# Blocks of 64 rows for the expert slots, half-size row moves, and another order of the expert tasks in a fused two-block model on one core

## The chip, the cores and the metric

The kernel runs on one core of a Trainium2 chip. The metric is the device time of one execution in microseconds (us). TensorE is PE in the profile (PEld: its weight loads), VectorE is DVE, ScalarE is ACT, GpSimd is POOL, and SyncE is SP, which here issues the weight loads.

## The reference

256 tokens of 1024 numbers pass through a first block (a mixer of sliding-window attention and gated linear attention, then a gated feed-forward part with a short convolution), and through a second block (a pooling mixer, a dense SwiGLU part, a state-space mixer, and a mixture of experts), all in float32. The change touches the last part only:

```python
t = h.reshape(b * l, d)                              # 256 tokens x 1024
logits = jnp.matmul(t, w_router).astype(jnp.float32) # 8 experts
top_val, top_idx = lax.top_k(logits, TOP_K)          # two experts for each token
gates = jax.nn.softmax(top_val, axis=-1)
...
for e in range(N_EXPERTS):                           # w_gate, w_up: 1024 x 3584; w_down: 3584 x 1024
    y_e = swiglu(t, w_gate[e], w_up[e], w_down[e]).astype(jnp.float32)
    out = out + combine[:, e:e + 1] * y_e            # combine: the gate of a token for e, or 0
```

The result is added to the residual, and a last norm follows.

## The kernel before

**Weights.** All weights come as units of 1 MB (128 partitions x 2048 numbers). SP loads a unit into one of six buffers `raw`; ACT rounds it to `w_hi`, DVE makes the rest `w_lo` = raw - w_hi, and PE multiplies with both parts. A buffer of `raw` comes free when DVE has made `w_lo` (the semaphore `lo_done`); there are three pairs of `w_hi` and `w_lo` (a fourth in small tasks), which come free when PE has used them (`unit_used`). Each engine has its own list of instructions, written out by hand, and semaphores order them between engines.

**Tasks.** Only the chosen experts of a token are computed. The kernel sorts tokens by expert into tasks of at most 128 or at most 64 rows, on the chip, since the counts depend on the data. Experts are split so that three of them have a large task (128 rows): expert 0 and the two others with most tokens. What they have over 128 rows, and the other experts, go into small tasks of 64 rows. A task loads the whole weights of its expert: 42 units. In a large task PE makes three products for each piece of weights (`mm3`); in a small one the high and the low half of 64 tokens lie side by side as 128 rows, and PE makes two (`mm2`). With the data of the runs there are eight tasks, three large and five small. Task 0 is expert 0's large one, and starts before the router's table is known. The small tasks follow, and the two other large ones come last (`n_next`, `n_last`). The engines read the number of tasks from `tasks` into registers, and run the small ones in a loop.

**Slots.** `slot_rows` in HBM has 128 rows for each of up to 16 tasks, with the token's number and its gate in each; a small task uses 64 of its 128. It is first filled with the number of an empty token. DVE works out the row of each token in `slots` (between the splits of task 0), the position list in `positions` and the list of tasks in `task_table`; POOL scatters token numbers and gates to `slot_rows` and reads the table back as `slot_tab`.

**Row moves, all issued by POOL.** `next_rows` gathers the 128 tokens of the next task from `token_rows` while the present task runs; PE transposes them near its end (`turn_rows`). When a task's result is complete, its 128 rows are stored to `result_rows`. During the last task, both results of each token are gathered from `result_rows` by position. Long before, at about 274 us, while the first feed-forward part runs, POOL fills all of `result_rows` (2048 rows) from 128 empty rows of `token_rows`, in one copy from HBM to HBM (L746).

The lines of the rows: L907 are SP's loads, L253 and L262 the splits in halves (large tasks and all earlier parts), L1462 and L2368 whole splits (small tasks), L269 to L271 `mm3`, L275 and L276 `mm2`, L2826 and L2829 the products of the feed-forward part, L1174 ACT's copies out of it, L3079 `turn_rows`, L2303 the low half of a product, L787 the reading of the slot table, L798 `next_rows`' gather.

## Time and profile before

| | us |
|---|---|
| median of 3 runs (lowest, highest) | 1787.6 (1787.14, 1790.38) |
| the profiled execution | 1786.82 |
| its span | 1785.1 |

The span is from the first to the last instruction; the time of the profiled execution is 1.7 us more. Mean granted TensorE clock: 0.989 of full speed. The first block takes up to about 400 us, the second block's parts before the experts up to about 870, the eight tasks the rest.

A row of a timeline gives start, length, engine, line, operation, what it writes and reads, how many instructions are merged in it, and in brackets how long the engine was idle before it and what ended that. A row of waits gives who waited for whom, with the total, the number of times and the longest.

### The profile page before, as it was taken

Reading aid. Unit: us, or ns where it says so; the run is one execution under the profiler, and the core shown is the slowest. Engines: PE = TensorE matmul, PEld = TensorE weight load, DVE = VectorE, ACT = ScalarE, POOL = GpSimd, SP = SyncE. Lnnn points to the kernel's source line nnn. Section 1 sums busy time; section 2 is a strip of 40 time slices with the busy share of each in tenths; the row PEclk is TensorE's granted clock in tenths of the full one; section 3 lists DMA queues with packets and bytes.
Section 4 is the critical chain, followed back from the end, with each engine's and each line's share of the span. In section 5 each row is a group of like instructions: output and inputs, shape, how many; then the busy total and the mean of one; then the engine's idle time right before and its main releaser. Section 6 shows DMA issues by size and latency. Waiting matters only on the chain.

```text
span 1785.1 us, 25176 instructions
## 1 busy us (share of the span) xinstructions
PE 1709.8 (96%) x8774; PEld 1432.4 (80%) x8774; DVE 1465.9 (82%) x1653; ACT 1254.0 (70%) x1490; POOL 188.0 (11%) x230
## 2 busy tenths in 40 slices
PE   9999998999999999999999998998999989999998
PEld 7888887888888899988877776776777777788886
DVE  6686775778766688857799899999999999999997
ACT  6655664556644576666677888888888888877776
POOL 2040050000000000132034100202012020000100
PEclk9999999999999999999999999999999999999999
DMA  9433459754555545433599999999999999999994
GB/s 337 149 111 135 159 199 281 269 197 151 184 193 188 167 165 190 157 127 107 205 349 383 382 421 406 424 422 420 424 420 423 421 420 425 404 396 365 410 383 182
DMA packets 176181, 515.45 MB, mean 289 GB/s; under 512 B 10964, under 2 KB 58450, under 8 KB 161634
## 3 DMA queue, kind: packets, MB, share of 16 engines
q1 hardware_dynamic: 172146, 493.08, 73.2%
q0 software_dynamic: 3808, 21.01, 3.2%
q8 instruction: 51, 0.84, 0.2%
q14 instruction: 32, 0.26, 0.0%
q10 hardware_dynamic: 144, 0.26, 0.0%
HBM read 508.01 MB, written 14.70 MB: 293 GB/s over the span
## 4 chain that ended last, share of the span: by engine, by line
PE 64%; DVE 14%; DMA 10%; issue 7%; ACT 5%; POOL 0%; DVEq 0%; ACTq 0%; SPq 0%; POOLq 0%
PE ps L269 14%; PE ps L271 14%; PE ps L270 14%; PE ps L2826 8%; DVE w_lo L2368 6%; DMA raw<-in_moe_w_gate_dram 5%; PE ps L2829 4%; DMA raw<-in_moe_w_up_dram 3%; DVE w_lo L262 3%; DMA raw<-in_w_ffn_in_dram 2%; DVE w_lo_more L2368 2%; ACT w_hi L1462 2%; PE ps L275 2%; PE ps L276 2%; PE ps L3226 1%
## 5 line engine op out<-in xcount | busy, mean ns | idle before, releaser
L262 DVE TENSOR_TENSOR w_lo<-raw,w_hi 128x1024 fp32r<-128x1024 f32 x517 | 612.0, 1233 | 87.3 <-ACT w_hi L253 85.3
L253 ACT ACTIVATE w_hi<-raw 128x1024 fp32r<-128x1024 f32 x518 | 518.9, 1057 | 169.2 <-PE ps L271 150.8
L2368 DVE TENSOR_TENSOR w_lo<-raw,w_hi 128x2048 fp32r<-128x2048 f32 x165 | 372.3, 2286 | 32.8 <-ACT w_hi L1462 31.6
L1462 ACT ACTIVATE w_hi<-raw 128x2048 fp32r<-128x2048 f32 x165 | 313.7, 1915 | 52.4 <-PE ps L276 23.5
L269 PE MATMUL ps<-w_hi,a 128*128 128x512 f32 (+1 forms) x656 | 259.6, 396 | 3.4 <-DVE w_lo L262 2.3
L271 PE MATMUL ps<-w_hi,a 128*128 128x512 f32 (+1 forms) x656 | 254.3, 388 | 0.0
L270 PE MATMUL ps<-w_lo,a 128*128 128x512 f32 (+1 forms) x656 | 253.8, 387 | 0.0
L2826 PE MATMUL ps<-a,w_hi 128*128 128x512 f32 x704 | 223.1, 398 | 6.9 <-DVE w_lo L262 6.9
L275 PE MATMUL ps<-w_hi,a 128*128 128x512 f32 x420 | 177.3, 422 | 14.6 <-DVE w_lo L2368 12.9
L269 PE MATMUL ps<-w_hi,a_hi 128*128 128x512 f32 (+1 forms) x440 | 170.8, 388 | 2.4 <-DVE w_lo L262 2.1
L276 PE MATMUL ps<-w_lo,a 128*128 128x512 f32 x420 | 170.6, 406 | 0.0
L271 PE MATMUL ps<-w_hi,a_lo 128*128 128x512 f32 (+1 forms) x440 | 169.6, 386 | 0.0
L270 PE MATMUL ps<-w_lo,a_hi 128*128 128x512 f32 (+1 forms) x440 | 169.6, 385 | 0.0
L2829 PEld LDWEIGHTS ps<-a,w_lo 128*128 128x128 f32 x704 | 133.3, 189 | 31.5
L269 PEld LDWEIGHTS ps<-w_hi,a 128*128 128x128 f32 x656 | 123.3, 188 | 31.6 <-issue 4.3
L271 PEld LDWEIGHTS ps<-w_hi,a 128*128 128x128 f32 x656 | 123.1, 188 | 25.7
L270 PEld LDWEIGHTS ps<-w_lo,a 128*128 128x128 f32 x656 | 123.3, 188 | 23.4
L2829 PE MATMUL ps<-a,w_lo 128*128 128x256 f32 x704 | 139.1, 279 | 0.0
L275 PEld LDWEIGHTS ps<-w_hi,a 128*128 128x128 f32 x420 | 83.1, 198 | 45.8 <-DVE w_lo L2368 28.9
L2826 PEld LDWEIGHTS ps<-a,w_hi 128*128 128x128 f32 x704 | 109.5, 190 | 8.6 <-DVE w_lo L262 7.1
L1174 ACT ACTIVATE arena<-ps 128x256 f32<-128x256 f32 x88 | 28.9, 381 | 109.5 <-PE ps L2829 109.5
L275 PE MATMUL ps<-w_hi,a_hi 128*128 128x512 f32 x240 | 96.2, 401 | 8.3 <-DVE w_lo L2368 7.5
(450 smaller groups left out, 2700.6 us busy)
## 6 DMA issues: line engine op xcount, KB each, us to landing
raw<-in_moe_w_gate_dram SPq DMA_DIRECT2D x112, 1024.0 KB, 9.1
raw<-in_moe_w_up_dram SPq DMA_DIRECT2D x112, 1024.0 KB, 9.0
raw<-in_moe_w_down_dram SPq DMA_DIRECT2D x112, 1024.0 KB, 9.8
raw<-in_ssd_w_in_dram SPq DMA_DIRECT2D x24, 1024.0 KB, 5.1
raw<-in_w_ffn_in_dram SPq DMA_DIRECT2D x22, 1024.0 KB, 5.1
raw<-in_w_in_dram SPq DMA_DIRECT2D x21, 1024.0 KB, 6.7
raw<-in_w_ffn_out_dram SPq DMA_DIRECT2D x11, 1024.0 KB, 5.0
raw<-in_dense_w_gate_dram SPq DMA_DIRECT2D x11, 1024.0 KB, 5.2
```

The costliest lines, as they stand in the source:

```text
L253: nc.scalar.activation(w_hi[:, u % SPL, part], raw[:, u % RAW, part], ACT.Copy).then_inc(hi_done, 1)
L262: last = nc.vector.tensor_tensor(w_lo[:, u % SPL, part], raw[:, u % RAW, part], w_hi[:, u % SPL, part].bitcast(F32), ALU.subtract)
L269: nc.tensor.matmul(o, lh, rh, start=start, stop=False, skip_group_check=True)
L270: nc.tensor.matmul(o, lh, rl, start=False, stop=False, skip_group_check=True)
L271: return nc.tensor.matmul(o, ll, rh, start=False, stop=stop, skip_group_check=True)
L275: nc.tensor.matmul(o, l, rh, start=start, stop=False, skip_group_check=True)
L276: return nc.tensor.matmul(o, l, rl, start=False, stop=stop, skip_group_check=True)
L1174: last = nc.scalar.activation(dst[:, fc, :], ps[bank + fc][:, S:2 * S], ACT.Copy)
L1462: nc.scalar.activation(small_part(u, True), raw[:, (M0 + u) % RAW, :], ACT.Copy).then_inc(hi_done, 2)
L2368: nc.vector.tensor_tensor(small_part(u, False), raw[:, (M0 + u) % RAW, :], small_part(u, True).bitcast(F32), ALU.subtract).then_inc(lo_don ...
L2826: nc.tensor.matmul(ps[bank + fc][:, :], w_hi[:, slot, cols], a0_hl[:, kc].rearrange("p a s -> p (a s)"), start=(kc == 0), stop=False, skip ...
L2829: last = nc.tensor.matmul(ps[bank + fc][:, 0:S], w_lo[:, slot, cols], a0_hi[:, kc, :], start=False, stop=(kc == DC - 1), skip_group_check= ...
```

## The change

1. **Packing.** `slot_rows` and `result_rows` have 19 blocks of 64 rows instead of 16 of 128: a small task takes one block, a large one two. `slot_tab` has two numbers for each of 19 windows of 128 rows that begin 64 rows apart; it is read by two copies, the second shifted by a block into the upper 64 partitions. The fill of `result_rows` copies 19 times 64 rows.
2. **Row moves.** A small task's rows are gathered as 64, and its result is stored as 64. Before each gather stands an addition of one column on POOL, and one more before the last gathers.
3. **Order of tasks.** Large, small, large, the other small ones, large: tasks 0, 2 and the last are large. Task 1 and 2 are written out; the loop has one round less.
4. **Table work.** `slots` and `task_table` become pieces (`slots_small`, `slots_large`, `slots`, `task_large`, `task_small`, `task_match`, `task_table`), most of them called behind single splits (`behind`). The formulas differ, since rows are packed otherwise and the order of tasks is another.

Its core (the same renamings for ACT, and the new table formulas beside the first, are left out):

```diff
+WINDOWS = MAX_TASKS + 3
...
-        slot_rows = nc.dram_tensor("slot_rows", (MAX_TASKS * P, 2), F32).ap()
-        result_rows = nc.dram_tensor("result_rows", (MAX_TASKS * P, D), F32).ap()
+        slot_rows = nc.dram_tensor("slot_rows", (WINDOWS * HALF, 2), F32).ap()
+        result_rows = nc.dram_tensor("result_rows", (WINDOWS * HALF, D), F32).ap()
...
-                pool.dma_start(result_rows.rearrange("(i p) d -> i p d", p=P),
-                               bcast(token_rows[S:S + P, :], 0, MAX_TASKS)).then_inc(y_out, 16)
+                pool.dma_start(result_rows.rearrange("(i p) d -> i p d", p=HALF),
+                               bcast(token_rows[S:S + HALF, :], 0, WINDOWS)).then_inc(y_out, 16)
...
-                pool.dma_start(slot_tab.rearrange("p (i c) -> p i c", c=2),
-                               slot_rows.rearrange("(i p) c -> p i c", p=P)).then_inc(tab_out, 16)
+                for n in range(2):
+                    windows = slot_tab[n * HALF:(n + 1) * HALF].rearrange("p (i c) -> p i c", c=2)
+                    pool.dma_start(windows[:, 0:WINDOWS - n], slot_rows[n * HALF:WINDOWS * HALF, :].rearrange(
+                        "(i p) c -> p i c", p=HALF)).then_inc(tab_out, 16)
...
+                def next_rows(i, window, n):
+
+                    pool.wait_ge(tab_out, 48 + 32 * T)
+                    nc.gpsimd.tensor_copy(next_idx, slot_tab[:, window]).then_inc(rows_idx, 2)
                     pool.wait_ge(rows_out, 32)
+                    pool.wait_ge(rows_idx, 2 * i)
+                    nc.gpsimd.tensor_tensor(pad[:, 64:65], pad[:, 65:66], pad[:, 66:67], ALU.add)
+                    nc.gpsimd.indirect_dma_start(m_row[0:n], None, token_rows,
+                                                 bass.IndirectOffsetOnAxis(ap=next_idx[0:n], axis=0)).then_inc(rows_in, 16)
+
+                def store_rows(i, rows, n):
+
                     pool.wait_ge(m_yhi, 2 * i + 2)
-                    pool.dma_start(result_rows[bass.ds(i * P, P), :], y_row).then_inc(y_out, 16)
+                    pool.dma_start(result_rows[rows, :], y_row[0:n]).then_inc(y_out, 16)
                     pool.wait_ge(y_out, i * 16 + 32)
+
+                next_rows(1, slice(4, 5), HALF)
+                store_rows(0, slice(0, P), P)
+                next_rows(2, slice(6, 7), P)
+                store_rows(1, slice(2 * HALF, 3 * HALF), HALF)
+                next_rows(3, slice(10, 11), HALF)
+                store_rows(2, slice(3 * HALF, 5 * HALF), P)
+                with pool.Fori(0, n_loop) as r:
+                    next_rows(r + 4, bass.ds(r * 2 + 12, 1), HALF)
+                    store_rows(r + 3, bass.ds(r * HALF + 5 * HALF, HALF), HALF)
+                next_rows(n_last, bass.ds(n_last * 2 + 4, 1), P)
+                store_rows(n_final, bass.ds(n_final * HALF + 2 * HALF, HALF), HALF)
+                nc.gpsimd.tensor_tensor(pad[:, 67:68], pad[:, 65:66], pad[:, 66:67], ALU.add)
...
+                def slots_small():
+
+                    C.link(nc.vector.tensor_tensor(base, end, parts, ALU.subtract))
+                    C.link(nc.vector.tensor_scalar(base, base, float(HALF), HALF - 1.0, ALU.mult, ALU.add))
+                    C.link(nc.vector.tensor_tensor(by_expert(row), by_expert(rho), bcast(base, 1, T), ALU.add))
+                    C.link(nc.vector.tensor_scalar(shift, row, 2.0 * HALF - 0.5, 2.0 * HALF, ALU.is_gt, ALU.mult))
+                    C.link(nc.vector.scalar_tensor_tensor(row, row, float(HALF), shift, ALU.add, ALU.add))
...
-                def wide_step_lo(i, j, added=None):
+                def wide_step_lo(i, j, added=None, behind={}):
...
                     for u in range(gate_u + 2, up_u + 2):
                         split_lo(dve, M0 + u, 7 * i)
+                        behind.get(u, lambda: None)()
...
-                wide_step_lo(0, 0, slots)
+                wide_step_lo(0, 0, None, {7: slots_small, 9: slots_large, 11: slots})
                 positions()
-                wide_step_lo(0, 1, task_table)
+                wide_step_lo(0, 1, None, {17: task_large, 19: task_small, 21: task_match})
+                task_table()
                 wide_step_lo(0, 2)
...
                 task(0, True)
                 small_head(1)
                 pe.wait_ge(r_tab, 1)
...
-                with pe.Fori(1, n_small) as i:
+                small_task(1)
+                project(0, ps[2], 7 * 2, 2)
+                project(2, ps[6], 7 * 2)
+                pe.wait_ge(m_yhi, 2 * 2)
+                task(2, True)
+                small_head(3)
+                with pe.Fori(3, n_final) as i:
                     small_task(i)
                     small_head(i + 1)
-                small_task(n_small)
-                project(0, ps[2], 7 * n_next, n_next)
-                project(2, ps[6], 7 * n_next)
-                pe.wait_ge(m_yhi, 2 * n_next)
-                task(n_next, True)
+                small_task(n_final)
                 project(0, ps[2], 7 * n_last, n_last)
```

How the instructions stand, at three places. First POOL, at about 262 to 274 us, before:

```order
L732 DMA arena<-in_pool_scale_dram 128x1024
L735 DMA token_rows<-pad 2048x1x64
L737 MEMSET slot_io 128x32
L738 IOTA slot_io 128x16
L740 IOTA slot_io 128x4
L743 DMA slot_rows<-slot_io 128x16x2
L746 DMA result_rows<-token_rows 16x8x16384
```

and after the change:

```order
L733 DMA arena<-in_pool_scale_dram 128x1024
L736 DMA token_rows<-pad 2048x1x64
L738 MEMSET slot_io 128x38
L739 IOTA slot_io 128x19
L741 IOTA slot_io 128x4
L744 DMA slot_rows<-slot_io 64x19x2
L747 DMA result_rows<-token_rows 19x4x16384
```

The last row is the fill: 16 times 8 pieces of 16384 numbers before, 19 times 4 after.

Then VectorE in the first wide step of task 0 (L262, after the change L263, are splits; two rows make a unit), before:

```order
L262 TENSOR_TENSOR w_lo<-raw,w_hi 128x1024 x8
L2303 TENSOR_TENSOR a_lo<-ps,a_hi 128x4x128
L262 TENSOR_TENSOR w_lo<-raw,w_hi 128x1024 x8
L2313 TENSOR_TENSOR arena<-arena,ps 128x512 x2
L2254 TENSOR_TENSOR arena<-arena 128x8
L2255 TENSOR_SCALAR arena<-arena 128x8
L2256 TENSOR_SCALAR arena<-arena 128x8
L2257 SCALAR_TENSOR_TENSOR arena<-arena 128x8
L2258 SCALAR_TENSOR_TENSOR arena<-arena 128x8
L2259 TENSOR_TENSOR arena<-arena 128x48
L2260 TENSOR_REDUCE arena<-arena 128x16
L2261 TENSOR_SCALAR arena<-arena 128x16
```

and after:

```order
L263 TENSOR_TENSOR w_lo<-raw,w_hi 128x1024 x4
L2284 TENSOR_TENSOR arena<-arena 128x8
L2285 TENSOR_SCALAR arena<-arena 128x8
L2286 TENSOR_TENSOR arena<-arena 128x16
L2287 TENSOR_SCALAR arena<-arena 128x16
L2288 SCALAR_TENSOR_TENSOR arena<-arena 128x16
L263 TENSOR_TENSOR w_lo<-raw,w_hi 128x1024 x4
L2292 TENSOR_SCALAR arena<-arena 128x1
L2293 TENSOR_SCALAR arena<-arena 128x8
L2294 TENSOR_SCALAR arena<-arena 128x8
L2295 SCALAR_TENSOR_TENSOR arena<-arena 128x8
L2354 TENSOR_TENSOR a_lo<-ps,a_hi 128x4x128
```

The operations on 128x8 and 128x16 are table work. Before, all twelve stand behind the two products (128x512 x2) and ahead of the next unit; after, five stand behind the first two units of the step, four behind the next two, four further on.

Last POOL in task 0, from the scatters to the gather for the second task, before:

```order
L784 DMA slot_rows<-slot_io,slot_idx 2048x2 x4
L787 DMA slot_io<-slot_rows 128x16x2
L790 TENSOR_LOAD tasks
L790 ISA x2
L801 UNCONDITIONAL_BRANCH
L795 ISA
L795 COPY slot_idx<-slot_io 128x1
L798 DMA arena<-token_rows,slot_idx 128x1024
```

and after:

```order
L785 DMA slot_rows<-slot_io,slot_idx 1216x2 x4
L790 DMA slot_io<-slot_rows 64x19x2
L790 DMA slot_io<-slot_rows 64x18x2
L793 TENSOR_LOAD tasks
L793 ISA x2
L794 TENSOR_LOAD tasks
L794 ISA x2
L795 TENSOR_LOAD tasks
L795 ISA x2
L800 CAST slot_idx<-slot_io 128x1
L803 TENSOR_TENSOR pad<-pad 128x1
L804 DMA arena<-token_rows,slot_idx 64x1024
```

The table is read by two copies, three values are loaded instead of one, and an addition stands between the copy of the indices and the gather, which is of 64 rows.

## Rows read from the trace of the kernel before

**Rows 1.** the page, part 1: busy us, share, instructions.

```profile
PE 1709.8 (96%) x8774; PEld 1432.4 (80%) x8774; DVE 1465.9 (82%) x1653; ACT 1254.0 (70%) x1490; POOL 188.0 (11%) x230
```

**Rows 2.** stretches of the experts: us, busy by engine, PEclk, DMA share, GB/s.

```profile
872.00:1000.00 128.00, 123.83 (x568) 102.04 (x567) 118.95 (x153) 98.76 (x114) 33.47 (x25) 1.00 0.92 346
1000.00:1110.00 110.00, 100.21 (x464) 79.14 (x462) 100.83 (x57) 93.97 (x70) 4.55 (x3) 0.97 1.01 405
...
1217.00:1324.00 107.00, 97.88 (x455) 77.87 (x455) 99.60 (x57) 90.72 (x69) 12.47 (x3) 0.97 1.02 422
...
1538.00:1657.00 119.00, 118.96 (x541) 98.71 (x540) 108.84 (x104) 93.14 (x103) 4.25 (x4) 1.00 0.99 386
```

**Rows 3.** waits of PE, 255 to 345: us in total, times, longest.

```profile
PE ps L2826 <- DVE w_lo L262: 6.9, 1, 6.9
```

**Rows 4.** timeline of ACT: start us, us, what, count, idle before.

```profile
274.50 0.66 ACT L1174 ACTIVATE arena<-ps 128x256 f32<-128x256 f32 x2 [3.55 <-PE ps L2829]
...
291.09 0.66 ACT L1174 ACTIVATE arena<-ps 128x256 f32<-128x256 f32 x2 [3.55 <-PE ps L2829]
...
308.91 2.00 ACT L253 ACTIVATE w_hi<-raw 128x1024 fp32r<-128x1024 f32 x2 [11.59 <-DMA raw<-in_w_ffn_in_dram]
...
333.70 0.66 ACT L1174 ACTIVATE arena<-ps 128x256 f32<-128x256 f32 x2 [3.55 <-PE ps L2829]
```

**Rows 5.** DMA issues, 270 to 275: count, KB each, us from issue to landing.

```profile
raw<-in_w_ffn_in_dram SPq DMA_DIRECT2D x1, 1024.0 KB, 38.1
...
result_rows<-token_rows POOLq DMA_DIRECT2D x1, 35.1
```

**Rows 6.** DMA queues, 280 to 305 (q0: POOL's): packets, MB, share.

```profile
q0 software_dynamic: 124, 8.13, 97.0%
q1 hardware_dynamic: 311, 0.49, 8.2%
```

**Rows 7.** stretches of the first feed-forward part, columns as in rows 2.

```profile
305.00:320.00 15.00, 8.09 (x34) 6.76 (x33) 8.43 (x14) 8.32 (x12) 0.00 (x0) 0.77 0.92 328
```

**Rows 8.** waits of PE, 862 to 1006.

```profile
PE ps L269 <- DVE w_lo L262: 3.9, 2, 1.9
```

**Rows 9.** timeline of PE: turning rows, then tasks' first matmuls.

```profile
980.75 1.03 PE L3079 MATMUL ps<-cst,arena 128*128 128x128 f32 x8
...
997.96 0.39 PE L275 MATMUL ps<-w_hi,a 128*128 128x512 f32 x1
...
1106.08 0.50 PE L275 MATMUL ps<-w_hi,a 128*128 128x512 f32 x1
...
1427.29 0.50 PE L275 MATMUL ps<-w_hi,a 128*128 128x512 f32 x1
...
1535.85 0.50 PE L269 MATMUL ps<-w_hi,a 128*128 128x512 f32 x1
...
1654.98 0.39 PE L269 MATMUL ps<-w_hi,a 128*128 128x512 f32 x1
```

**Rows 10.** timeline of DVE in task 0: the first of each lump.

```profile
910.08 0.15 DVE L2254 TENSOR_TENSOR arena<-arena 128x8 f32<-128x8 f32 x1
...
941.56 0.27 DVE L2271 TENSOR_TENSOR arena<-arena,cst 1x128 f32<-1x128 f32 x1
```

**Rows 11.** waits of DVE, 882 to 950.

```profile
DVE a_lo L2303 <- ACT a_hi L1385: 1.0, 2, 0.6
DVE w_lo L262 <- ACT w_hi L253: 0.2, 1, 0.2
```

**Rows 12.** timeline of POOL in task 0.

```profile
962.01 1.21 POOL L787 DMA_DIRECT2D slot_io<-slot_rows  x1 [5.79 <-DMA slot_rows<-slot_io,slot_idx]
...
971.18 1.16 POOL L798 DMA_INDIRECT arena<-token_rows,slot_idx  x1 [0.81 <-POOL slot_idx L795]
```

**Rows 13.** DMA issues, 970 to 973: count, us to landing.

```profile
arena<-token_rows,slot_idx POOLq DMA_INDIRECT x1, 8.6
```

More of the change, by code:

```diff
@@ L45 @@
 MAX_TASKS = 16
-N_BEFORE, N_LAST, N_TASKS = 16, 19, 20
+WINDOWS = MAX_TASKS + 3
+N_LOOP, N_PAST, N_FINAL, N_LAST, N_TASKS = 16, 17, 19, 20, 21
 UC = 2048
@@ L2151, in _ @@
                 first_e = R[18][:, NE:2 * NE]
-                order, large, rest, parts, end, place, base, swap = (m_tab[:, NE * k:NE * (k + 1)] for k in range(8))
+                order, large, rest, parts, end, place, base, second = (m_tab[:, NE * k:NE * (k + 1)] for k in range(8))
                 over, key = m_tab[:, 64:128].rearrange("p (e f) -> p e f", e=NE), m_tab[:, 128:136]
                 step, over4 = m_tab[:, 136:140], m_tab[:, 160:192].rearrange("p (e k) -> p e k", k=4)
-                rho, whole, left, back = (m_tab[:, 192 + 16 * k:208 + 16 * k] for k in range(4))
-                over3 = m_tab[:, 256:304].rearrange("p (n k) -> p n k", k=3)
+                rho, row, wide_row, shift = (m_tab[:, 192 + 16 * k:208 + 16 * k] for k in range(4))
+                last_row = m_tab[:, 256:257]
+                ordinal, not_two = m_tab[0:1, 272:288], m_tab[0:1, 288:304]
+                later = m_tab[0:1, 304:305]
                 below, same = (m_tab[0:1, 320 + 128 * k:448 + 128 * k].rearrange("p (i e) -> p i e", e=NE) for k in range(2))
@@ new lines, in slots_large @@
+                def slots_large():
+                    C.link(nc.vector.tensor_scalar(last_row, end[:, NE - 1:NE], float(HALF), 4.0 * HALF, ALU.mult, ALU.add))
+                    C.link(nc.vector.tensor_scalar(second, order, 1.0, last_row, ALU.is_equal, ALU.mult))
+                    C.link(nc.vector.tensor_scalar(place, order, 0.5, 3.0 * HALF, ALU.is_lt, ALU.mult))
+                    C.link(nc.vector.scalar_tensor_tensor(place, place, P - 1.0, second, ALU.add, ALU.add))
+                def slots():
+                    C.link(nc.vector.tensor_tensor(by_expert(wide_row), by_expert(rho), bcast(place, 1, T), ALU.add))
+                    C.link(nc.vector.scalar_tensor_tensor(row, rho, 0.5, row, ALU.is_gt, ALU.mult))
+                    C.link(nc.vector.scalar_tensor_tensor(wide_row, rho, 0.5, wide_row, ALU.is_lt, ALU.mult))
+                    C.link(nc.vector.tensor_tensor(R[5], row, wide_row, ALU.add))
@@ new lines, in task_large, with task_small @@
+                def task_large():
+                    C.link(nc.vector.tensor_scalar(later, end[0:1, NE - 1:NE], 2.0, None, ALU.add))
+                    C.link(nc.vector.tensor_scalar(second[0:1], order[0:1], 1.0, later, ALU.is_equal, ALU.mult))
+                    C.link(nc.vector.tensor_scalar(place[0:1], order[0:1], 0.5, 2.0, ALU.is_lt, ALU.mult))
+                    C.link(nc.vector.tensor_tensor(place[0:1], place[0:1], second[0:1], ALU.add))
+                def task_small():
+                    C.link(nc.vector.tensor_tensor(ordinal, iota_row[0:1, 0:MAX_TASKS], ordinal, ALU.subtract))
+                    C.link(nc.vector.tensor_tensor(below, bcast(end[0:1, :], 1, MAX_TASKS), bcast(ordinal, 2, NE), ALU.is_lt))
+                    C.link(nc.vector.tensor_reduce(small_e, below, AX.X, ALU.add))
@@ L2270, in task_table, with task_match @@
+                def task_match():
                     row = iota_row[0:1, 0:MAX_TASKS]
[L2271 to L2272 removed]
                     C.link(nc.vector.tensor_tensor(same, bcast(place[0:1, :], 1, MAX_TASKS), bcast(row, 2, NE), ALU.is_equal))
@@ L2337, in wide_step_lo @@
                         split_lo(dve, M0 + u, 7 * i)
+                        behind.get(u, lambda: None)()
                     product(i, 2 * j + 1)
@@ L2343, in wide_step_lo, with task_end_lo @@
                         split_lo(dve, M0 + u, 7 * i)
-                def task_end_lo(i, more, first=False, n=P):
+                def task_end_lo(i, more, gate_at, n=P):
                     split_lo(dve, M0 + 36, 7 * i)
@@ L2352, in task_end_lo @@
                         tokens_lo(i + 1, n)
-                    dve.wait_ge(tab_out, 32 + 32 * T)
-                    nc.vector.tensor_copy(m_gate, slot_tab[:, 1:2] if first else slot_tab[:, bass.ds(i * 2 + 1, 1)]).then_inc(m_gates, 1)
+                    dve.wait_ge(tab_out, 48 + 32 * T)
+                    nc.vector.tensor_copy(m_gate, slot_tab[:, gate_at]).then_inc(m_gates, 1)
                     for u in range(38, 44 if more else 42):
                         split_lo(dve, M0 + u, 7 * i)
-                def task_lo(i, more):
-                    for j in range(3):
-                        wide_step_lo(i, j)
-                    task_end_lo(i, more)
                 def whole_lo(i, *units):
```

114 lines of the change are left out of this document (53 added, 61 removed).

## The prediction

> **What bounds the kernel now.** First the page: TensorE is busy for 1709.8 of 1785.1 us, the others clearly less [rows 1]. So an edit pays where TensorE waits, or where it runs no faster than its data come. The table of stretches gives the second kind. In the five small tasks TensorE is busy for 98 to 100 us of 107 to 110, while the DMA share is 1.01 to 1.02 at 405 to 422 GB/s: the transfers set the pace. In the large task from 1538 to 1657 TensorE is busy for 118.96 us of 119 at 386 GB/s: there it sets the pace itself [rows 2]. The waits give the first kind. Before the experts, the longest single wait that I look at is 6.9 us, near 310 us, for a weight part from VectorE [rows 3]. Followed back: ScalarE, which makes the part before VectorE, had waited 11.59 us for the weights to land, until 308.91 [rows 4]. That load took 38.1 us from issue to landing, and beside it ran the copy that fills result_rows, 35.1 us [rows 5]. The reader is to see that the last two end together.
>
> **The fill of result_rows.** This is a side effect of the packing, and the largest term. The tensor shrinks from 16 x 128 rows to 19 x 64, with 4 KB a row: from 8.39 MB to 4.98 MB.
> How the fill hurts: from 280 to 305 us it moved 8.13 MB in 124 packets, so 65.6 KB each, and the weights' queue got only 311 packets and 0.49 MB in 25 us [rows 6]. A weight load needs every engine, and on each it stands behind packets of the fill. One packet costs 25 us x 16 engines x 0.97 / 124 = 3.1 us of one engine. The least it can cost is 65.6 KB at the 422 GB/s / 16 of the small tasks: 2.5 us [rows 2].
> What it costs: equal steps of the feed-forward loop begin at 274.50 and 291.09, so 16.59 us apart. The mark at 333.70 is the third step after 274.50: 59.20 us later, where three steps of 16.59 are 49.77 [rows 4]. The loss is 9.4 us: 6.9 of waiting, and 2.5 for the low clock behind it (granted 0.77 of full speed over 305 to 320, which is a mixture of 1.2 and 2.4 GHz) [rows 7].
> How much goes: before, each engine has 128 / 16 = 8 packets. After, there are 76. Spread evenly that is 5 on an engine at most: 3 x 3.1 = 9.3 us earlier, more than the 6.9 of the wait, so all 9.4 us go. If whole blocks of 64 rows stay on one engine, 19 blocks lie on ten engines with two each, 8 packets again. With six engines idle the packet costs between 2.5 and 3.1 us, so the end is 5 to 0 us earlier. At 5 a wait of 1.9 is left; VectorE already makes TensorE wait 1.9 us twice in the first task [rows 8], and the granted clock of that task stays at 1.00 [rows 2], so the 2.5 would go too: 7.5 us. I take 8.5, between the two spreads; the bounds are 0 and 9.4. Nothing takes the wait's place: the loads queued behind this one are freed with it, and ScalarE wants them later than this one.
>
> **Half rows for small tasks.** A gather or a store of 64 rows moves 0.26 MB less. That counts only while transfers set the pace. In the new order, task 1 still has a store of 128 (task 0's) and a gather of 128 (for task 2): nothing. The half moves of task 1 itself and the gather for task 3 fall into task 2, which is bound by TensorE: nothing. Task 3 saves one, 4 and 5 two each, 6 one: six halves, 1.57 MB. At 422 GB/s [rows 2] that is 3.7 us. The bound from the other side is 0, if the small tasks were held by something else; VectorE is busy 99.6 us of 107 there, so there are 7 us of room for a saving of 1.2 a task.
>
> **The order of tasks.** TensorE passes from task to task at 997.96, 1106.08, then three tasks to 1427.29, 1535.85 and 1654.98 [rows 9]. So the first small task took 108.12 us, the middle ones 107.07 on average, the last 108.56, the large one 119.13 without a wait. The excess of 1.05 belongs to a small task that follows a large one: ScalarE splits whole units only after it has copied the large result out. The 1.49 I put on a small task before a large one, where 128 rows are gathered. Both kinds of change of task now happen twice: +2.5 us, bounds 0 and +5 (none of it if these excesses are chance, twice it if the second change finds the queues worse placed). A large task after a small one costs the same as one after a large one, since TensorE sets its pace.
>
> **Table work in task 0.** VectorE does a lump of twelve operations from 910.08 and one of eight from 941.56, 0.15 to 0.3 us each [rows 10]; behind each, TensorE waits 1.9 us, 3.9 together [rows 8]. The change makes 13 and 14 operations of them, 0.2 us each, in pieces of 0.8 to 1 us behind the splits. But VectorE waits only 1.2 us in all between 882 and 950 (0.2 of it for split parts) [rows 11]: it is the bound of this stretch, and moving its work gives back idle time only. The seven operations more cost 1.1 us, of which four come late, where there is room. Gain 0.9 us at most.
> Against it stands POOL's chain. The slot table is now read by two copies instead of one (1.21 us to issue, now at 962.01), and a small addition stands before the gather, which was issued at 971.18 [rows 12] and landed 8.6 us later [rows 13], at 979.8. TensorE turned the rows at 980.75 [rows 9]: 1 us of room (the scatters before the table's copy move with the splits that POOL waits for, by under 1 us either way). A gather that is 1.2 + 0.5 later and, with half the rows, 1 us quicker to land, comes at 980.5, and TensorE is there 0.9 earlier: it waits 0.6 to 1. The wait holds everything, since all four transposes and the down products are queued behind it. The step as a whole: +0.3 us, bounds -0.9 and +3.
> The dozen rows added before task 0, the wider slot table and the value loads lie beside other work: 0. The gathers of results at the end are issued some 3 us later against the last task, and are read over 8 us after they landed: 0.
>
> **Sum.** -8.5 - 3.7 + 2.5 + 0.3 = -9.4 us. The profiled execution took 1786.8 us (span 1785.1), so it would be 1777.4; the median of the runs shown is 0.8 above it: 1778.
>
> **Rivals.**
> (a) The fill ends no earlier (8 packets on an engine at 3.1 us). For it: a first dimension of 19 does not divide among 16 engines. Against: the packets' price at sixteen engines is above the 2.5 us, so fewer engines should be quicker. Time: 1787.6 - 0.9 = 1787.
> (b) Slower, by one mechanism: the whole fill goes through one engine. What decides is how POOL's copy is shared out when its first dimension, 19, has no common divisor with 16. No row shows such a copy: the first dimensions of POOL's copies before are 16, 128 and 2048. If so, 76 packets of 2.5 to 3.1 us run one after another: 190 to 236 us from 280, to 470 to 516 instead of 309. Every weight load has a share on that engine and gets about one packet in for each of the fill [rows 6], so the feed-forward stops at about 308, as now, and goes on some 5 us after the fill's end. That is 161 to 207 us more: 1787.6 + 165 - 0.9 = about 1952, up to 1994. It decides as soon as fewer than about seven engines share the fill (76 / 7 x 2.5 = 27 us).
> The Trainium skill has the rule for this (DMA: Bandwidth & Descriptors, "Why a DMA increments its semaphore by 16 and not by 1"): a copy is spread over the largest number of engines up to 16 that divides the slowest dimension of both sides, which for 19 is one. By it the sum is (b). The same section makes an exception for some direct copies issued by GpSimd, which go by the rounded-up share for each engine; that is the ten engines above. The trace of before agrees with either, since 16 divides evenly.
> (c) The order and the late gather cost their upper bounds, +5 and +3, and the halves give 2: -8.5 - 2 + 8 = -2.5, so 1785.
>
> **How the numbers follow.** Forecast, the fill spread over ten or more engines and the wait gone: 0.67, at 1778, itself 1774 to 1783. (a) 0.10. (b) 0.17, since the kind of copy is unseen and the rule speaks for it, while the exception to the rule speaks against; the trace itself leaves it open. (c) 0.06. The range is 1773 to 1788; above it lies (b), left out. This kernel's runs can tell a change from none at about 0.2%, 3.6 us: faster takes the forecast and half of (c), 0.70; the same takes (a) and the other half of (c), 0.13; slower is (b), 0.17.
>
> **What would show it.** The fill's landing: under 30 us right, 35 is (a), about 200 is (b). TensorE's wait at 310 gone or under 2 us, and granted clock 1.0 from 305 to 320. Middle small tasks at 105.8 us; the small task after the second large one 107.5 to 108. In task 0 no wait of 1.9, and one of about 1 before the transposes near 980. I am wrong on the main step if the fill lands early and the feed-forward is no shorter, and on the model of the small tasks if they stay at 107 us.

## The result and the profile after

The changed kernel takes 1934.12 us (median of 4 runs, 1929.8 to 1938.1), the kernel before 1788.34 us (4 runs, 1787.14 to 1790.38): a ratio of 1.081, 95% interval 1.079 to 1.084. It is slower by 146 us, where 1778 us was forecast. What came is rival (b), which had a chance of 0.17 and a price of 1952.

The strips of the profile's page show at a glance where the time goes: TensorE's busy tenths and the granted clock over the span of 1928.1 us, a digit for 48 us.

```profile
PE   9999996002999999999999999999999999999998
...
PEclk9999998555999999999999999999999999999999
```

TensorE does next to nothing in the eighth and ninth slice and little in the tenth, and its clock falls to 0.5. The waits of TensorE from 255 to 500 us answer to [rows 3], where the longest was 6.9; columns as there.

```profile
PE ps L2879 <- DVE w_lo L263: 146.8, 1, 146.8
PE ps L270 <- DVE w_lo L263: 4.2, 1, 4.2
```

The timeline of ScalarE answers to [rows 4]: equal steps of the feed-forward loop, and the parts that were late.

```profile
274.31 0.66 ACT L1192 ACTIVATE arena<-ps 128x256 f32<-128x256 f32 x2 [3.55 <-PE ps L2882]
...
290.89 0.66 ACT L1192 ACTIVATE arena<-ps 128x256 f32<-128x256 f32 x2 [3.55 <-PE ps L2882]
...
468.70 2.00 ACT L254 ACTIVATE w_hi<-raw 128x1024 fp32r<-128x1024 f32 x2 [152.48 <-DMA raw<-in_w_ffn_in_dram]
...
479.82 0.66 ACT L1192 ACTIVATE arena<-ps 128x256 f32<-128x256 f32 x2 [1.83 <-PE ps L2882]
...
496.42 0.66 ACT L1192 ACTIVATE arena<-ps 128x256 f32<-128x256 f32 x2 [3.55 <-PE ps L2882]
```

From 274.31 to 290.89 a step takes 16.58 us, and the one from 479.82 to 496.42 takes 16.60. The mark at 479.82 is the third after 274.31, as 333.70 was after 274.50: 205.5 us where three steps are 49.8. The loss is 155.7 us; before it was 9.4. The difference, 146.3 us, is the result (145.8 between the medians, 143.0 between these two profiles). ScalarE waited 152.48 us for one weight load.

Between these rows stand two more, the load on which ScalarE worked last before the standstill, and TensorE's first product behind it:

```profile
313.68 2.00 ACT L254 ACTIVATE w_hi<-raw 128x1024 fp32r<-128x1024 f32 x2 [12.68 <-DMA raw<-in_w_ffn_out_dram]
```

```profile
472.20 1.22 PE L2879 MATMUL ps<-a,w_hi 128*128 128x512 f32 x2 [146.84 <-DVE w_lo L263]
```

So TensorE waited 4.2 us near 313, worked on the unit that had landed, and stood still from 325.4 to 472.2.

The DMA issues near 270 answer to [rows 5]:

```profile
raw<-in_w_ffn_in_dram SPq DMA_DIRECT2D x1, 1024.0 KB, 9.5
...
result_rows<-token_rows POOLq DMA_DIRECT2D x1, 195.8
```

The queues of the same kernel from 320 to 460, in the middle of the standstill, answer to [rows 6]:

```profile
q0 software_dynamic: 57, 3.74, 6.2%
q1 hardware_dynamic: 57, 0.06, 0.1%
```

The fill lands after 195.8 us instead of 35.1. In 140 us the fill's queue moves 57 packets of 65.6 KB, that is 2.46 us each, and takes 6.2% of 16 engines' time: one engine, always busy. The weights' queue gets 57 packets in the same time, one between two of the fill's. The prediction read that ratio, one to one, from [rows 6]; the counts there are 311 weight packets beside 124 of the fill, two and a half to one. The load that ScalarE waited for landed only with the end of the fill, so it had a share on that engine.

The stretches of the standstill and of its end, columns as in [rows 2] and [rows 7]:

```profile
320.00:440.00 120.00, 5.36 (x19) 3.95 (x17) 0.00 (x0) 0.00 (x0) 0.00 (x0) 0.53 0.06 27
440.00:480.00 40.00, 7.80 (x34) 6.72 (x35) 9.95 (x14) 8.65 (x13) 0.00 (x0) 0.55 0.42 144
```

From 320 to 440 the granted clock was 0.53 of full speed on average, so nearly all of it at the lower of the two levels, 1.2 GHz. Of the 155.7 us lost, 151.0 are the two waits; the other 4.7 are put down to the slower matmuls behind each of them.

### The profile page after: what moved, and what is told of

Read it like the earlier page. It is cut to its first block, busy times and chain, and to the rows that moved or that the text cites. A ratio compares the mean times of both kernels' runs of the same rounds, so it can differ in the third digit from the quotient of the medians.

```text
span 1928.1 us, 24853 instructions
## 1 busy us (share of the span) xinstructions
PE 1711.1 (89%) x8774; PEld 1430.6 (74%) x8774; DVE 1466.4 (76%) x1662; ACT 1254.2 (65%) x1490; POOL 201.7 (10%) x239
## 2 busy tenths in 40 slices
DMA packets 176680, 509.47 MB, mean 264 GB/s; under 512 B 12168, under 2 KB 59638, under 8 KB 162182
## 4 chain that ended last, share of the span: by engine, by line
PE 56%; DVE 15%; DMA 9%; another core or an unknown queue 8%; issue 6%; ACT 4%; DVEq 0%; POOL 0%; ACTq 0%; SPq 0%; POOLq 0%
PE ps L270 12%; PE ps L272 12%; PE ps L271 12%; PE ps L2879 7%; DVE w_lo L2415 6%; DVE w_lo L263 4%; PE ps L2882 3%; DMA raw<-in_moe_w_gate_dram 3%; DMA raw<-in_moe_w_up_dram 2%; ACT w_hi L1480 2%; DMA raw<-in_moe_w_down_dram 2%; DMA raw<-in_w_ffn_out_dram 2%; DVE w_lo_more L2415 2%; PE ps L276 1%
## 5 line engine op out<-in xcount | busy, mean ns | idle before, releaser
L263 DVE TENSOR_TENSOR w_lo<-raw,w_hi 128x1024 fp32r<-128x1024 f32 x517 | 611.4, 1231 | 247.0 <-ACT w_hi L254 245.1
L254 ACT ACTIVATE w_hi<-raw 128x1024 fp32r<-128x1024 f32 x518 | 518.9, 1057 | 321.2 <-DMA raw<-in_w_ffn_in_dram 152.5
L2879 PE MATMUL ps<-a,w_hi 128*128 128x512 f32 x704 | 222.7, 398 | 146.8 <-DVE w_lo L263 146.8
L2879 PEld LDWEIGHTS ps<-a,w_hi 128*128 128x128 f32 x704 | 109.2, 190 | 148.7 <-DVE w_lo L263 147.3
L2415 DVE TENSOR_TENSOR w_lo_more<-raw,w_hi_more 128x2048 fp32r<-128x2048 f32 x45 | 102.7, 2283 | 0.5 <-ACT w_hi_more L1480 0.3
```

What stands on the lines that cost most here:

```text
L254: nc.scalar.activation(w_hi[:, u % SPL, part], raw[:, u % RAW, part], ACT.Copy).then_inc(hi_done, 1)
L263: last = nc.vector.tensor_tensor(w_lo[:, u % SPL, part], raw[:, u % RAW, part], w_hi[:, u % SPL, part].bitcast(F32), ALU.subtract)
L2415: nc.vector.tensor_tensor(small_part(u, False), raw[:, (M0 + u) % RAW, :], small_part(u, True).bitcast(F32), ALU.subtract).then_inc(lo_don ...
L2879: nc.tensor.matmul(ps[bank + fc][:, :], w_hi[:, slot, cols], a0_hl[:, kc].rearrange("p a s -> p (a s)"), start=(kc == 0), stop=False, skip ...
```

## Experiments: the fill

All kernels are compared with the kernel before on the same chip. "The fill in 16" is this edit, made in the changed kernel; it fills the same 1216 rows, in 16 pieces of 304 KB instead of 19 of 256 KB:

```diff
-pool.dma_start(result_rows.rearrange("(i p) d -> i p d", p=HALF),
-               bcast(token_rows[S:S + HALF, :], 0, WINDOWS)).then_inc(y_out, 16)
+pool.dma_start(result_rows.rearrange("(i p) d -> i p d", p=76),
+               bcast(token_rows[S:S + 76, :], 0, 16)).then_inc(y_out, 16)
```

> The changed kernel with one edit: its fill of result_rows, the same 1216 rows, is written as 16 pieces of 76 rows instead of 19 of 64. Theory (the copy's first dimension decides over how many engines it is spread; 19 puts it on one): 16 engines with five packets each, landing under 30 us instead of 195.8, the wait of 146.8 us on TensorE gone, time 1778 (1774 to 1783), which is the sum of the prediction. Rival (the 146 us come from another part of the change: order, half rows or the table): the time stays near 1930. Second rival (the rest of the change is worth nothing): 1788 less the fill's 9.4, so 1779, told apart by the same fill in the kernel before.

Measured: 1777.39 us (12 runs, 1775.11 to 1790.2), ratio 0.996 (0.9943 to 0.9977). The fill lands after 21.4 us and no wait of TensorE is left between 255 and 345. The stretch that answers to [rows 7]:

```profile
305.00:320.00 15.00, 15.00 (x81) 12.82 (x80) 10.66 (x21) 8.93 (x14) 0.00 (x0) 1.00 0.60 211
```

The issue that answers to [rows 5]:

```profile
result_rows<-token_rows POOLq DMA_DIRECT2D x1, 4864.0 KB, 21.4
```

TensorE is busy for all 15 us at a granted clock of 1.00. The packets of this fill are smaller, 128 of 38.9 KB (eight for each of 16 engines) where the changed kernel has 76 of 65.5 KB, so this run alone does not tell the first dimension from the size of a packet; 38 and 76 pieces below, with packets of 65.5 KB, do. The whole loss is the fill's, and without it the sum of the prediction (1777.4, or 1778) comes out. How far that is luck, the later runs tell.

The same fill in the kernel before, with result_rows cut to 1216 rows:

```diff
-result_rows = nc.dram_tensor("result_rows", (MAX_TASKS * P, D), F32).ap()
+result_rows = nc.dram_tensor("result_rows", (1216, D), F32).ap()
...
-n_last = pool.value_load(tasks[0:1, N_LAST:N_LAST + 1], min_val=3, max_val=MAX_TASKS - 1)
+n_last = pool.value_load(tasks[0:1, N_LAST:N_LAST + 1], min_val=3, max_val=9)
```

> The kernel before with result_rows cut to 1216 rows (its tasks use 1024) and the fill written as 16 pieces of 76 rows. Theory: only the 9.4 us at 300 to 333 go, so 1779 (1778 to 1788, the upper end if the fill takes as long as before). With the changed kernel with the same fill beside it, the difference is the worth of order, half rows and table work: 0.9 us by the prediction's terms (-3.7 + 2.5 + 0.3).

Measured: 1777.59 us (5 runs, 1776.76 to 1778.74), ratio 0.9944 (0.9931 to 0.9956). The 9.4 us of [rows 4] go: the third step is now 49.8 us after the first mark, and between the medians it is 9.2 us. The rest of the change (order, half rows, table work) is then worth 0.2 us between the medians, which is nothing that these runs can tell.

The same kernel with p=64 and 19 in that fill, as the change writes it, and nothing else of the change:

> The kernel before with result_rows cut to 1216 rows and the fill written as 19 pieces of 64 rows, as the changed kernel has it; nothing else of the change. Theory (first dimension 19 gives one engine): landing after 190 to 200 us, TensorE waits some 147 us, time about 1788.3 + 147 = 1935. Rival (the slot table, value loads or another part of the change slow it): the fill lands within 35 us and the time is 1779 to 1788.

Measured: 1935.24 us (2 runs), ratio 1.0827 (1.0808 to 1.0845). The issue that answers to [rows 5]:

```profile
result_rows<-token_rows POOLq DMA_DIRECT2D x1, 194.2
```

The fill's queue in this kernel from 320 to 460:

```profile
q0 software_dynamic: 57, 3.74, 6.2%
```

The shape of one copy, in the old kernel, makes the whole loss. The rival, that another part of the change makes it, falls.

Then the shape itself, in the changed kernel; only the 76 and 16 of the edit above take other values. 76 pieces of 16 rows are one packet each:

> The changed kernel with the fill written as 76 pieces of 16 rows. Theory A (as many engines as the largest number up to 16 that divides the first dimension: 4): 19 packets on each of four engines at 2.6 us, landing after 49 us, that is 14 us later than in the kernel before, time about 1788.3 + 14 - 1 = 1801. Theory B (the rounded-up share, 76 / 16 = 5 pieces an engine, which would make 16 engines, and a special case for fewer than 20 pieces): landing under 30 us, time 1778. Theory C (any first dimension that 16 does not divide goes to one engine): landing 196 us, time 1934.

Measured: 1777.79 us (4 runs, 1774.22 to 1782.19), ratio 0.995 (0.9934 to 0.9967); the fill lands after 20.8 us. Theories A and C fall for this shape, and B stands. With 38 pieces of 32 rows, two packets each:

> The changed kernel with the fill written as 38 pieces of 32 rows (128 KB each, so two packets a piece). Theory A (the largest number up to 16 that divides the first dimension): two engines, 38 packets each at 2.58 us, landing after 98 us, time about 1837 (1934 less 98). It has not held for 76 pieces of one packet each, which landed after 20.8 us where four engines would need 49. Theory B (a first dimension of more than 16 that is even, or anything but 19, is spread evenly): 21 us, 1778. Theory C (a piece that is more than one packet is spread only where 16 divides): one engine, 196 us, 1934.

Measured: 1840.09 us (1 run, the kernel before 1785.28 beside it). The issue:

```profile
result_rows<-token_rows POOLq DMA_DIRECT2D x1, 101.1
```

The fill's queue in this kernel from 320 to 360:

```profile
q0 software_dynamic: 33, 2.16, 12.5%
```

33 packets in 40 us at 12.5% of 16 engines: two engines, each with a packet every 2.42 us. Theory A, which failed at 76, gives this to 3 us (101.1 against 98, 1840 against 1837). So two more shapes of pieces that are a packet or less:

> The changed kernel with the fill written as 152 pieces of 8 rows (32 KB each). Theory A: 8 engines, 19 pieces of 32 KB each, about 25 us if a packet is 32 KB and half the price. Theories B and C (pieces of one packet are joined or spread over all): 20 to 21 us. Time 1778 by each; what tells them apart is the number and size of the packets and the landing.

Measured: 1785.77 us (1 run), the fill lands after 23.7 us, and TensorE does not wait for it. By the landing alone theory A would stand (it said 25).

> The changed kernel with the fill in four copies of 19 pieces of 16 rows (64 KB, one packet each). Theory A, and C if it is the 19: one engine, 76 packets of 2.6 us, landing of the last after 196 us, time 1934. If what put 19 pieces on one engine was that a piece is more than one packet: landing after about 21 us (up to 26 with two packets on an engine for each copy), time 1778 to 1780.

```diff
+for q in range(3):
+    pool.dma_start(result_rows[304 * q:304 * q + 304, :].rearrange("(i p) d -> i p d", p=16),
+                   bcast(token_rows[S:S + 16, :], 0, 19)).then_inc(rows_out, 16)
+pool.dma_start(result_rows[912:1216, :].rearrange("(i p) d -> i p d", p=16),
+               bcast(token_rows[S:S + 16, :], 0, 19)).then_inc(y_out, 16)
```

(The waits for the last store of token_rows count the three copies too.) Measured: 1782.11 us (1 run); the four land after 18.2 us (median; the last after 27.8), and TensorE does not wait. So it is not the 19 by itself. How many engines took part, the fill's queue from 280 to 292 tells: 76 pieces,

```profile
q0 software_dynamic: 63, 2.82, 73.6%
```

152 pieces,

```profile
q0 software_dynamic: 116, 3.15, 76.9%
```

and four copies of 19:

```profile
q0 software_dynamic: 134, 2.75, 63.3%
```

The shares are 73.6, 76.9 and 63.3% of 16 engines, so at least 12, 13 and 11 engines were at it. By theory A it would be four, eight (50% at most), and one for each copy. The traces also hold each packet with its start and length: of the fill's packets at most one is under way at any time with 19 pieces, two with 38, and sixteen with every other shape. All kernels of this part together:

| first dimension x piece | fill's packets | at once | landing, us | packets under 512 B in the whole kernel | kernel, us |
|---|---|---|---|---|---|
| 19 x 256 KB | 76 of 65.5 KB | 1 | 195.8 | 12168 | 1934 |
| 38 x 128 KB | 76 of 65.5 KB | 2 | 101.1 | 11560 | 1840 (one run) |
| 16 x 304 KB | 128 of 38.9 KB | 16 | 21.4 | 11028 | 1777 |
| 76 x 64 KB | 76 of 65.5 KB | 16 | 20.8 | 11032 | 1778 |
| 152 x 32 KB | 152 of 32.8 KB | 16 | 23.7 | 11036 | 1786 (one run) |
| 4 copies of 19 x 64 KB | 76 of 65.5 KB | 16 | 18.2 (median) | 11128 | 1782 (one run) |

Why 1786 and 1782 there, with no wait at the fill, is told below.

The fifth column tells more. The fill in 16 has the fewest small packets. Against it 19 pieces have 1140 more, which is 15 times 76, and 38 have 532 more, which is 14 times 38; all of them are of 4 bytes. That fits fifteen engines that get an empty packet for each of the 76 on the one, and fourteen that get one for each of the 38 on each of two. With 76 pieces there are 4 more, with 152 there are 8: 16 x 5 - 76 and 16 x 10 - 152. The four copies of 19 have 100 more: 48 are the closing packets of the three added copies (16 of 4 bytes for each copy), and the 52 left are 4 x (16 x 2 - 19). So these three shapes fit a rounded-up share of 5, 10 and 2 pieces for each engine. That the small packets fill up the shorter lists is read from the counts alone.

The rule that the prediction cited stands for the shapes whose pieces are larger than 64 KB. It is from the Trainium skill (DMA: Bandwidth & Descriptors, "Why a DMA increments its semaphore by 16 and not by 1"): the largest number of engines up to 16 that divides the slowest dimension. The traces agree at 19 (one engine) and 38 (two), and nothing at 16 speaks against it. The exception of the same section for some direct copies of GpSimd, by the rounded-up share, does not hold for 19 or 38 pieces of more than a packet: it would have made ten and thirteen engines. But it fits the counts of the three shapes whose pieces are one packet (76, 152, and the four of 19, which by it go over ten engines for each copy). What in the copy decides between the two was not tested beyond these six shapes.

## Experiments: the rest of the change

Three kernels take back one part each, all with the fill in 16. The mark is the row in which TensorE turns the rows of the next task [rows 9], which is there once a task.

> The changed kernel with the fill in 16 pieces once more, as the reference for three kernels that take back one part each and run beside it. 1777.4 as measured before, within 2 us. From the marks where TensorE turns the rows of a task: 110.0 us to the second mark, 117 to 118.4 over the large task, 108 behind it, 106.3 to 107.3 for small tasks in the middle.

Measured: 1778.95 us (6 runs, 1774.67 to 1783.95). The intervals between marks: 109.97, 118.53, 115.96, 106.64, 107.79, 106.78. One is 8 us off the expectation (115.96 instead of 108); a slow stretch of the transfers lies in it, as told in the last section.

> The changed kernel with the fill in 16 pieces, and the table work of task 0 put back into two lumps behind the two steps. By the prediction VectorE is the bound there and moving its work is worth 0.9 us at most, a late gather costs 0.6 to 1: the mark of turned rows in task 0 comes 0 to 1 us later than without the lumps. By the traces since (waits of 3.9 us before, 1.5 after; mark at 972.3 before and 969.8 after with equal fills) it comes 2.4 us later, TensorE waits twice, about 1.9 us each, and the kernel takes 2.4 us more.

```diff
-wide_step_lo(0, 0, None, {7: slots_small, 9: slots_large, 11: slots})
+wide_step_lo(0, 0, lambda: (slots_small(), slots_large(), slots()))
...
-wide_step_lo(0, 1, None, {17: task_large, 19: task_small, 21: task_match})
-task_table()
+wide_step_lo(0, 1, lambda: (task_large(), task_small(), task_match(), task_table()))
```

Measured: 1779.77 us (6 runs, 1778.91 to 1782.33), 0.8 above the one before, which these runs cannot tell from nothing; the marks can. The wait that answers to [rows 8], with lumps:

```profile
PE ps L270 <- DVE w_lo L263: 5.4, 2, 3.3
```

and spread (the first run with the fill in 16):

```profile
PE ps L270 <- DVE w_lo L263: 1.5, 4, 0.6
```

The mark of turned rows in task 0, with lumps:

```profile
974.18 1.04 PE L3131 MATMUL ps<-cst,arena 128*128 128x128 f32 x8
```

and spread:

```profile
969.78 1.03 PE L3132 MATMUL ps<-cst,arena 128*128 128x128 f32 x8
```

Spreading saves 3.9 us of waiting and moves the mark by 4.4 (0.2 of it stands already at 863, before task 0). The kernel before, with the fill in 16, has its mark at 972.30: the new tables in lumps cost 1.9 us, and spread they gain 2.5 (0.3 of it stands at 863 already). Both expectations had the sign, neither the size (0 to 1, and 2.4).

> The changed kernel with the fill in 16 pieces, and small tasks that gather 128 rows and store 128 rows again (the last small task's store stays at 64, since behind it are rows that must stay zero; rows beyond a task's own are overwritten by the next task's store). By the prediction 1.2 us more for each small task in the middle (107.5 instead of 106.3) and 3 to 3.7 in all. Rival: the middle small tasks are 0.4 us longer or less (the traces of both kernels differ by 107.07 against 106.6), since half the rows is not half the time on the queues, and the sum is under 1.5 us.

```diff
-next_rows(r + 4, bass.ds(r * 2 + 12, 1), HALF)
-store_rows(r + 3, bass.ds(r * HALF + 5 * HALF, HALF), HALF)
+next_rows(r + 4, bass.ds(r * 2 + 12, 1), P)
+store_rows(r + 3, bass.ds(r * HALF + 5 * HALF, P), P)
```

(The same for tasks 1 and 3, which stand before the loop.) Measured: 1777.09 us (6 runs, 1775.45 to 1779.13), so the runs show no loss. The kernels with half rows had slow stretches in some of their runs, though, and the marks are less plain. The three middle small tasks take 106.67, 107.83 and 106.76 us between marks, 321.3 together. With half rows three such tasks take 321.2 (the second profile of the fill in 16, above), 320.3 (the fill in 76), 319.9 (the changed kernel with its own fill) and 318.3 (the old order, second profile): 0 to 1.0 us a task less. The task behind the second large one takes 110.33 with whole rows, and 107.7 to 108.6 in the seven profiles with half rows that have no slow stretch there. From the mark in task 0 to the end it is 806.9 us with whole rows, against 802.3 and 804.5 in the two profiles of half rows and this order without a slow stretch. So the half rows are worth nothing by the medians, and 2.4 to 4.6 us by these single profiles; it stays open.

> The changed kernel with the fill in 16 pieces, and the order of the kernel before: large, five small, large, large (packed slots, half rows and spread table work stay). By the prediction 2.5 us less (1.05 for one small task less behind a large one, 1.49 for one less in front of one): 1775. Rival (the excess belongs to the place and not to the change of task): the same time within 1 us.

The tables put the second large task behind the small ones again, and the programs of the engines follow:

```diff
-small_task(1)
-project(0, ps[2], 7 * 2, 2)
-project(2, ps[6], 7 * 2)
-pe.wait_ge(m_yhi, 2 * 2)
-task(2, True)
-small_head(3)
-with pe.Fori(3, n_final) as i:
+with pe.Fori(1, n_small) as i:
     small_task(i)
     small_head(i + 1)
-small_task(n_final)
+small_task(n_small)
+project(0, ps[2], 7 * n_next, n_next)
...
+task(n_next, True)
```

Measured: 1779.86 us (12 runs, 1772.93 to 1787.44), ratio 0.9957 (0.9938 to 0.9975), against 0.9949 (0.993 to 0.9967) of the new order beside it. That does not tell them apart. In its profile one task took 113.4 us instead of 107, so the kernel was run once more:

> The order of tasks of the kernel before in the changed kernel, fill in 16 pieces, once more, since in the first profile the transfers ran at 367 GB/s instead of 421 for 90 us. Where no such stretch falls into a small task: 802.3 less 1.5 to 2.5 us from the mark of turned rows in task 0 to the end, that is 800 to 801; rival (order is worth nothing): 802.3.

Measured: 1774.7 us (1 run). From the mark in task 0 (970.81) to the end of the span (1773.0) it is 802.2 us; in the profile of the changed kernel with its own fill it is 802.3 (1125.81 to 1928.1). There the small task behind the second large one took 108.16 us, and the three behind it 107.30, 106.28 and 106.33. So the excess of such a task is seen. But the last small task, in front of a large one, takes 106.33 there, where it takes 107.91 in the old order, so the new order gets back at its end most of what it pays in the middle. Over all the two orders come out equal in these two profiles, within 1 us; the changed kernel with the fill in 76, which has no slow stretch either, has 804.5, which is 2.3 more. The four fastest runs of the old order (1772.93 to 1774.12) lie 1.5 to 1.9 us below the four fastest of 18 of the new (1774.67 to 1775.6), which also speaks for a small cost of the new order. It stays open.

## Why the prediction was wrong

**The step that failed** is "If whole blocks of 64 rows stay on one engine, 19 blocks lie on ten engines with two each ... I take 8.5, between the two spreads", with its chance of 0.67. The spread was one engine, and TensorE stood still for 146.8 us. The text had the other case with its condition, and said that "the trace of before agrees with either, since 16 divides evenly". With nothing in the trace between them, one should not have had four times the chance of the other, and the one with the large price should have set the range.

**The rival's price** was right in kind: 76 packets, one after another, each with a weight packet behind it. A packet came every 2.46 us in the trace, just below the 2.5 to 3.1 that the rival worked with, because 2.5 us was a packet at the small tasks' rate for each engine, and the 3.1 were of sixteen engines at once. The fill's packets ran from 280 to 468, 188 us, just short of its 190 to 236. Its time was 1952, and 1934 came. With the low end of its price it would still be 1948, so the price explains 4 us of the 18. Most of the rest is the step "the feed-forward stops at about 308, as now": TensorE stood still only from 325.4, since one more unit had landed, and had done some 11 us of work by then that the rival counts as lost. "Fewer than about seven engines decide" holds as far as it was run: with two engines the kernel is 55 us slower. No fill on a number of engines between two and sixteen was run.

**How the fill hurts, and what a short one gives back.** Right. With 16 engines the 6.9 us of waiting and the 2.5 of low clock both went in both kernels (1786.8 to 1777.6 in the kernel before). The term was 8.5 in the sum, and the full 9.4 is what an even spread gives by the same step.

**Half rows: 3.7 us forecast, not settled.** The medians say 0, the single profiles without a slow stretch 2.4 to 4.6 us. The prediction's sign, middle small tasks at 105.8 us, did not come: with half rows they take 106.1 to 107.1 us on average, with whole rows 107.1, so the saving in them is 0 to 1.0 us a task where 1.2 was forecast.

**Order: +2.5 forecast, 0 to 2 measured.** The excess behind a large task is there the second time too (108.16, 107.76, 108.36, where the middle tasks take 106.2 to 107.8). The 1.49 in front of a large one is there in the old order (107.91 against 106.1) but not at the end of the new one (106.33 to 106.87), which the sum did not foresee.

**Table work: +0.3 forecast, -2.2 to -2.5 measured.** Two errors. The gain was capped at VectorE's idle time of 1.2 us in the stretch [rows 11]. The right cap was TensorE's wait of 3.9 [rows 8], of which 1.5 is left; the likely reason is that a delayed split is caught up behind 950, where VectorE has room. And the late gather did not come. The timeline of GpSimd in the changed kernel with the fill in 16:

```profile
933.41 1.25 POOL L785 DMA_INDIRECT slot_rows<-slot_io,slot_idx  x1 [0.31 <-issue]
934.97 1.91 POOL L785 DMA_INDIRECT slot_rows<-slot_io,slot_idx  x1 [0.30 <-issue]
...
957.23 1.01 POOL L800 CAST slot_idx<-slot_io 128x1 int32<-128x1 f32 x1 [8.04 <-DMA slot_io<-slot_rows]
...
959.54 1.78 POOL L804 DMA_INDIRECT arena<-token_rows,slot_idx  x1 [0.16 <-issue]
```

and in the kernel before with the fill in 16:

```profile
933.94 1.05 POOL L784 DMA_INDIRECT slot_rows<-slot_io,slot_idx  x1 [0.31 <-issue]
935.30 9.78 POOL L784 DMA_INDIRECT slot_rows<-slot_io,slot_idx  x1 [0.30 <-issue]
...
961.26 0.63 POOL L795 CAST slot_idx<-slot_io 128x1 int32 x1 [7.32 <-DMA slot_io<-slot_rows]
962.70 1.18 POOL L798 DMA_INDIRECT arena<-token_rows,slot_idx  x1 [0.81 <-POOL slot_idx L795]
```

The second scatter took 9.78 us before and 1.91 after. It began only when VectorE's lump had ended, and lay beside the eight splits that VectorE made behind it without a gap:

```profile
935.04 9.15 DVE L262 TENSOR_TENSOR w_lo<-raw,w_hi 128x1024 fp32r<-128x1024 f32 x8
```

In the spread kernel VectorE makes eight splits without a gap as well, from 932.52 to 941.7, and the scatters beside them take 1.9 us each. The kernel with lumps has such a long scatter as well, its third, and yet its gather is issued only 0.2 us after the spread one above:

```profile
935.54 7.52 POOL L785 DMA_INDIRECT slot_rows<-slot_io,slot_idx  x1 [0.30 <-issue]
...
959.76 1.44 POOL L804 DMA_INDIRECT arena<-token_rows,slot_idx  x1 [0.49 <-issue]
```

So the gather is issued 3.2 us earlier than in the kernel before, in spite of the second copy of the table and the addition, but not because the lumps are in pieces: the four scatters end 3.5 us earlier even with lumps (944.3 against 947.8), where the prediction had them move "by under 1 us either way". Why one scatter is long is open. The gather lands 9.0 us later, at 968.5, and the rows are turned at 969.78 without a wait for them.

The three small terms (-3.7, +2.5, +0.3: -0.9) came out as 0 to -4.6, 0 to 2 and about -2.5. By the medians their sum is -0.2. That 1777.4 us with an even spread is near the forecast of 1778 is a coincidence: none of the three is shown to have come out at its size.

## What to carry to other kernels

When a change touches the shape of a DMA, look at its first dimension before its bytes: a copy of 40% fewer bytes took 5.6 times as long, because 19 pieces of 256 KB went through one engine and 16 pieces did not. The weight loads, which are spread over all engines, stood behind the one copy that wasn't. Where two rules for such a shape can't be told apart in the trace and one costs 160 us, the range belongs to both, and writing the copy with 16 pieces costs nothing.

To bound a gain by a wait, take the wait of the engine that sets the end, not the idle time of the one that feeds it.

## What the runs showed besides

**Transfers have slower stretches.** In some executions they run 7 to 11% slower for 80 to 90 us, with the DMA engines as busy as ever. The stretch from 1460 to 1540 in the changed kernel with the fill in 16,

```profile
1460.00:1540.00 80.00, 71.81 (x322) 56.81 (x322) 69.66 (x41) 63.26 (x48) 0.00 (x0) 0.94 1.02 386
```

and with the fill in 76:

```profile
1460.00:1540.00 80.00, 73.69 (x338) 58.01 (x336) 73.35 (x43) 67.42 (x52) 0.58 (x1) 0.96 1.02 416
```

The stretch from 1220 to 1310 in two executions of one kernel, the old order; the first,

```profile
1220.00:1310.00 90.00, 78.06 (x370) 62.44 (x368) 77.22 (x44) 69.59 (x55) 12.28 (x3) 0.96 1.02 375
```

and the second:

```profile
1220.00:1310.00 90.00, 82.97 (x395) 66.18 (x395) 83.90 (x48) 76.38 (x60) 11.50 (x3) 0.98 1.02 420
```

The last columns are the DMA share and GB/s: 386 against 416, and 375 against 420, at a share of 1.02 each. In a small task that costs 4 to 8 us (111.15, 115.96, 113.4 instead of 107), and in five of the six profiles that have one the next task is 2 us longer as well (109.2 to 109.7). It came in six of the nine profiles of the changed kernel and its variants with a spread fill (the two of 1782 and 1786 in the table of fills are among them), at 1460 to 1540 in four of them, and in neither the profile of the kernel before nor the one with its fill in 16. It can explain why one such kernel has runs from 1773 to 1787. Its cause is open.

**The best kernel** of those run is the changed one with the fill in 16 or the kernel before with the same fill: 1777.4 and 1777.6 us, 0.5% under the kernel before. With 128 rows for the small tasks as well it is 1777.1, the same.
